# Weighting and summing two of the three w_ada blocks on VectorE instead of TensorE

## The reference

```python
c_act = jax.nn.silu(c)
mod = jnp.einsum('bd,dm->bm', c_act, w_ada[l]) + b_ada[l]
shift_m, scale_m, gate_m, shift_f, scale_f, gate_f = jnp.split(mod, N_MOD, axis=-1)
h = modulate(rms_norm(x, g_norm_mix[l]), shift_m, scale_m)
p = jnp.einsum('bsd,dk->bsk', h, w_in[l])
...
x = x + gate_m[:, None, :] * mix_out
h2 = modulate(rms_norm(x, g_norm_moe[l]), shift_f, scale_f)
moe_out = expert_choice_moe(h2, w_router[l], b_router[l], w_gate_e[l], w_up_e[l], w_down_e[l])
x = x + gate_f[:, None, :] * moe_out
```

## Time and profile before

| | us |
|---|---|
| median of three runs | 1432.08 (1430.69 to 1432.92) |
| the profiled execution | 1429.03 |
| its span | 1427.2 |
| TensorE busy | 1162.0 (81%) |
| VectorE busy | 322.9 (23%) |
| ScalarE busy | 246.1 (17%) |
| GpSimd busy | 87.7 (6%) |

### The profile page before, as it was taken

How to read it: one execution, slowest core, us unless ns; L and a number is a source line. 1 busy time by engine, 2 the same in 40 slices (tenths; PEclk the granted TensorE clock), 3 DMA queues, 4 the chain that set the end, 5 groups by cost and what they waited for, 6 DMA issues and landing times.

```text
span 1427.2 us, 16989 instructions
## 1 busy us (share of the span) xinstructions
PE 1162.0 (81%) x7070; PEld 634.3 (44%) x7071; DVE 322.9 (23%) x459; ACT 246.1 (17%) x355; POOL 87.7 (6%) x95
## 2 busy tenths in 40 slices
PE   4999999888778787777777778777787777996888
PEld 1789999533323133131222213213122223996777
DVE  1546446310000000000000000000000002666555
ACT  2423533100000000000000000000000003653644
POOL 2000000000000000000000000000000001421122
PEclk8999999697887968978787896888868889998989
DMA  9996884599999999999999999999999999742311
GB/s 333 379 361 240 265 299 174 228 421 421 422 422 421 422 421 422 422 422 422 422 422 422 422 422 422 422 422 422 422 422 422 422 422 373 242 143 89 119 64 55
DMA packets 116634, 496.33 MB, mean 348 GB/s; under 512 B 8140, under 2 KB 60772, under 8 KB 64116
## 3 DMA queue, kind: packets, MB, share of 16 engines
q1 hardware_dynamic: 114944, 490.37, 86.2%
q0 software_dynamic: 1296, 5.19, 1.1%
q10 hardware_dynamic: 356, 0.21, 0.1%
HBM read 494.70 MB, written 1.05 MB: 347 GB/s over the span
## 4 chain that ended last, share of the span: by engine, by line
DMA 45%; PE 36%; SPq 8%; DVE 4%; ACT 4%; issue 2%; POOL 0%; DVEq 0%; ACTq 0%
DMA ring<-in_w_gate_e 28%; SPq L463 8%; DMA ring<-in_w_down_e 8%; DMA ring<-in_w_up_e 7%; PE psum L556 7%; PE psum L557 6%; PE psum L558 6%; PE psum L823 6%; PE psum L804 4%; DMA ring<-in_w_in 3%; PE psum L850 2%; PE psum L624 1%; ACT ring_r L1035 1%; ACT arena L1165 1%; PE psum L675 1%
## 5 line engine op out<-in xcount | busy, mean ns | idle before, releaser
L823 PE MATMUL psum<-ring,arena 128*32 128x512 f32 x2048 | 314.6, 735 | 118.2 <-DMA ring<-in_w_gate_e 72.8
L850 PE MATMUL psum<-ring,arena 128*32 128x512 f32 x1024 | 233.0, 696 | 52.9 <-DMA ring<-in_w_down_e 38.8
L823 PEld LDWEIGHTS psum<-ring,arena 128*32 128x32 f32 x2048 | 57.3, 124 | 346.2 <-DMA ring<-in_w_gate_e 152.4
L850 PEld LDWEIGHTS psum<-ring,arena 128*32 128x32 f32 x1024 | 55.8, 121 | 220.9 <-DMA ring<-in_w_down_e 113.7
L556 PE MATMUL psum<-ring_r,ht_hi 128*128 128x256 f32 (+1 forms) x384 | 114.9, 299 | 10.9 <-DVE ht_lo L1289 7.8
L1285 DVE TENSOR_TENSOR ring_r<-ring,ring_r 128x2048 fp32r<-128x2048 f32 x43 | 101.9, 2394 | 74.0 <-ACT ring_r L1035 73.9
L556 PE MATMUL psum<-ht_hi,ring_r 128*128 128x256 f32 x384 | 109.3, 285 | 6.1 <-issue 6.1
L558 PE MATMUL psum<-ring_r,ht_lo 128*128 128x256 f32 (+1 forms) x384 | 113.2, 295 | 0.0
L557 PE MATMUL psum<-ring_r,ht_hi 128*128 128x256 f32 (+1 forms) x384 | 112.8, 294 | 0.0
L804 PEld LDWEIGHTS psum<-arena 128*128 128x128 f32 x544 | 99.9, 288 | 25.7 <-issue 24.7
L1035 ACT ACTIVATE ring_r<-ring 128x2048 fp32r<-128x2048 f32 x55 | 103.1, 1907 | 47.6 <-DMA ring<-in_w_in 30.5
(11 more groups left out here) (255 smaller groups left out, 958.0 us busy)
## 6 DMA issues: line engine op xcount, KB each, us to landing
ring<-in_w_gate_e SPq DMA_DIRECT2D x128, 1024.0 KB, 26.5
ring<-in_w_up_e SPq DMA_DIRECT2D x128, 1024.0 KB, 26.9
ring<-in_w_down_e SPq DMA_DIRECT2D x128, 1024.0 KB, 26.9
ring<-in_w_in SPq DMA_DIRECT2D x38, 1024.0 KB, 11.2
ring<-in_w_ada SPq DMA_DIRECT2D x24, 1024.0 KB, 11.0
ring<-in_w_conv_out SPq DMA_DIRECT2D x4, 1024.0 KB, 6.0
ring<-in_w_o SPq DMA_DIRECT2D x4, 1024.0 KB, 11.1
ring<-in_w_out SPq DMA_DIRECT2D x4, 1024.0 KB, 4.8
```

What stands on the lines that cost most here:

```text
L823: last = mm(psum[32 * g:32 * g + 32, b, :], cur[h][:, k, :], slot_in(s, g=4, n=512)[:, g, :], start=(k == 0), stop=(k == KD - 1), tile_pos ...
L850: last = mm(psum[32 * q:32 * q + 32, 2 + n, :], act_t[:, f % 4, (f // 4) * CAP:(f // 4 + 1) * CAP], w[:, kk, n * BANK:(n + 1) * BANK], sta ...
```

## The change

The eight slots of block 1 and of block 2 no longer go to PE. DVE multiplies each slot by its column of c_act (128 rows, one weight to a partition) and adds it to a running sum `ada_sum` of 128 x 2048 (`add_ada`): tensor_scalar for the first slot of a block, scalar_tensor_tensor in place for the seven others. It does so in unit u for the slots ahead of unit u+1, behind the splits of that unit and ahead of the emptying of its banks. PE waits at the head of unit u+1 until these additions are done (`ada_done`), and sums the 128 partitions of `ada_sum` once a block, by products with ones: `sum_row` (128x128 by 128x512) where a vector is needed as a row on all partitions, `sum_columns` (eight products with one column) where it is needed as columns. Block 1's sums stand ahead of c1's product; block 2's stand ahead of yb0's, but for one `sum_row` behind yb1. The step that makes scale_f moves on DVE from behind yb0's gating to ahead of it.

`ada_sum` takes one ring place, so arriving slots have 11 instead of 12 in the head. An ada slot is no longer released by itself: `others` adds it to the release of the first slot of the next product. The transposes of blocks 1 and 2, ACT's two copies ahead of them and the four small matmuls at L708 go.

```diff
@@ -45,7 +45,8 @@
 EXPERT_SLOTS = 24
 
 
-HEAD_PARTS, HEAD_RING = 4, RING - 4
+HEAD_PARTS, HEAD_RING = 4, RING - 5
+SUM_PLACE, HEAD_PART_ROOM = RING - 5, RING - 4
...
-        mod_rows = [area(5640, BANK), area(1536, BANK), area(2048, BANK)]
+        mod_rows = area(5640, BANK)
+        ada_sum = ring[:, SUM_PLACE, :]
...
-        part_place = {s: HEAD_RING + n % HEAD_PARTS for n, s in enumerate(head_split)}
+        part_place = {s: HEAD_PART_ROOM + n % HEAD_PARTS for n, s in enumerate(head_split)}
...
+        ada_step = {bk: n + 1 for n, bk in enumerate(bk for u in sorted(ADA_BEFORE) for bk in ADA_BEFORE[u])}
+
+        def ada_before(u):
+
+            since = max((v for v in range(u) if HEAD_UNITS[v][1]), default=-1)
+            return sum(len(ADA_BEFORE.get(v, ())) for v in range(since + 1, u + 1))
...
-            def transposed_product(s, u, act_parts):
+            def transposed_product(s, u, act_parts, others=0):
...
-                    last.then_inc(slot_used, 1)
+                    last.then_inc(slot_used, 1 if j else 1 + others)
...
+            def sum_columns(first, at):
+
+                for c in range(KD):
+                    last = mm(psum[:, 6, at + c:at + c + 1], ada_sum[:, first + c * P:first + (c + 1) * P], ones[:, 0:1], start=True, stop=True)
+                last.then_inc(ada_turned, 1)
+
+            def sum_row(first, to):
+
+                return mm(bank(to), ones, ada_sum[:, first:first + BANK], start=True, stop=True)
...
             for u, (name, slots) in enumerate(HEAD_UNITS):
                 for bk in ADA_BEFORE.get(u, ()):
-                    if bk == (1, 0):
-                        pe.wait_ge(mod_ready, 1)
-                    modulation(*bk, 3 + bk[0])
+                    pe.wait_ge(ada_done, ada_step[bk])
+                if (1, KD - 1) in ADA_BEFORE.get(u, ()):
+                    pe.wait_ge(mod_ready, 1)
+                    pe.wait_ge(gain_ready, 1)
+                    for n in range(2):
+                        sum_row(n * BANK, 4 + n).then_inc(gate_row_done, 1)
+                    sum_columns(D, 0)
+                if (2, KD - 1) in ADA_BEFORE.get(u, ()):
+                    sum_row(D + BANK, 7)
+                    sum_columns(0, KD)
...
-                    transposed_product(first_slot[name], u, (ht_hi, ht_lo))
+                    transposed_product(first_slot[name], u, (ht_hi, ht_lo), ada_before(u))
...
-                        end_first(last) if j == 0 else end_second(last, slots)
+                        end_first(last) if j == 0 else end_second(last, slots + ada_before(u))
...
-                    transposed_product(first_slot[name], u, (st_hi, st_lo))
-                    if name == "yb0":
-                        pe.wait_ge(gain_ready, 1)
-                        turn_modulation(1, 6)
-                        turn_modulation(2, 7)
+                    transposed_product(first_slot[name], u, (st_hi, st_lo), ada_before(u))
 
             pe.wait_ge(mod_ready, 2)
-            for g, b, first in ((0, 1, 0), (1, 2, 2)):
-                for n in range(2):
-                    r = 32 * (first + n)
-                    mm(bank(4 + 2 * g + n), ones[r:r + 1, :], mod_rows[b][r:r + 1, :], start=True, stop=True,
-                       tile_position=(r, 0)).then_inc(gate_row_done, 1)
+            sum_row(D, 6).then_inc(gate_row_done, 2)
...
-            def modulation_rows(b, from_bank):
-                act.wait_ge(slot_used, first_slot[f"ada{b}_{KD - 1}"] + 1)
-                f(mod_rows[b], bank(from_bank), ACT.Copy).then_inc(mod_rows_ready, 1)
-
-            modulation_rows(0, 4)
+            act.wait_ge(slot_used, first_slot[f"ada0_{KD - 1}"] + 1)
+            f(mod_rows, bank(4), ACT.Copy).then_inc(mod_rows_ready, 1)
...
-                if name == "yb0":
-                    modulation_rows(1, 4)
-                    modulation_rows(2, 5)
...
+            def summed_columns(n, q):
+                dve.wait_ge(ada_turned, n + 1)
+                link(V.tensor_tensor(mod_t[:, q:q + KD], psum[:, 6, n * KD:(n + 1) * KD], col[:, C_BADA + q:C_BADA + q + KD], ALU.add))
+
+            def add_ada(b, k):
+
+                s = first_slot[f"ada{b}_{k}"]
+                arrived(dve, s)
+                w = ring[:, place(s)[0], :]
+                if (b, k) == (2, 0):
+                    summed_columns(0, Q_SHIFT_F)
+                if k == 0:
+                    V.tensor_scalar(ada_sum, w, c_act[:, k:k + 1], None, ALU.mult).then_inc(ada_done, 1)
+                else:
+                    dve.wait_ge(ada_done, ada_step[b, k] - 1)
+                    V.scalar_tensor_tensor(ada_sum, w, c_act[:, k:k + 1], ada_sum, ALU.mult, ALU.add).then_inc(ada_done, 1)
...
                 split_ahead(head_ahead[u])
+                for bk in ADA_BEFORE.get(u + 1, ()):
+                    add_ada(*bk)
...
+                    if name == "yb0":
+                        summed_columns(1, Q_SCALE_F)
+                        V.scalar_tensor_tensor(mod_a[:, KD:2 * KD], mod_t[:, Q_SCALE_F:Q_SCALE_F + KD], 1.0, col[:, C_GMOE:C_GMOE + KD],
+                                               ALU.add, ALU.mult).then_inc(mod_ready, 1)
...
-                    if name == "yb0":
-                        modulation_columns(1, 6)
-                        modulation_columns(2, 7)
-                        V.scalar_tensor_tensor(mod_a[:, KD:2 * KD], mod_t[:, Q_SCALE_F:Q_SCALE_F + KD], 1.0, col[:, C_GMOE:C_GMOE + KD],
-                                               ALU.add, ALU.mult).then_inc(mod_ready, 1)
```

More of the change, by code:

```diff
@@ L269, in build @@
         gate_row_done, gate_row_ready = sem("gate_row_done"), sem("gate_row_ready")
+        ada_done, ada_turned = sem("ada_slots_summed"), sem("ada_sum_turned")
         squared, mean_ready, root_ready, scale_ready, xr_ready = (sem(n) for n in ("squared", "mean_ready", "root_ready", "scale_ready", "xr_ready"))
@@ L617, in turn_norm, with modulation @@
                     last.then_inc(norm_turned, 1)
-            def modulation(b, k, to):
-                s = first_slot[f"ada{b}_{k}"]
+            def modulation(k, to):
+                s = first_slot[f"ada0_{k}"]
                 arrived(pe, s)
@@ L626, in modulation, with turn_modulation @@
                 last.then_inc(slot_used, 1)
-            def turn_modulation(b, to):
-                pe.wait_ge(mod_rows_ready, b + 1)
+            def turn_modulation(to):
+                pe.wait_ge(mod_rows_ready, 1)
                 for c in range(4):
-                    last = nc.tensor.transpose(bank(to, c=4, m=P)[:, c, :], mod_rows[b][:, c * P:(c + 1) * P], ident)
+                    last = nc.tensor.transpose(bank(to, c=4, m=P)[:, c, :], mod_rows[:, c * P:(c + 1) * P], ident)
                 last.then_inc(mod_turned, 1)
+            def sum_columns(first, at):
[4 more added lines that the diff above has]
+                return mm(bank(to), ones, ada_sum[:, first:first + BANK], start=True, stop=True)
             pe.wait_ge(tables_loaded, 16)
@@ L647, in _ @@
                     nc.tensor.transpose(psum[:, 6, 0:5 + KD], vec2[0:5 + KD, :], ident[0:5 + KD, 0:5 + KD]).then_inc(gain_turned, 1)
-                modulation(0, k, 4)
-            turn_modulation(0, 5)
+                modulation(k, 4)
+            turn_modulation(5)
             for u, (name, slots) in enumerate(HEAD_UNITS):
                 for bk in ADA_BEFORE.get(u, ()):
-                    if bk == (1, 0):
-                        pe.wait_ge(mod_ready, 1)
-                    modulation(*bk, 3 + bk[0])
+                    pe.wait_ge(ada_done, ada_step[bk])
[8 more added lines that the diff above has]
+                    sum_columns(0, KD)
                 if name == "fourier_in":
@@ L1299, in split_norm, with modulation_columns @@
                     ins.then_inc(norm_lo, 1)
-            def modulation_columns(b, from_bank):
-                dve.wait_ge(mod_turned, b + 1)
+            def modulation_columns(from_bank):
+                dve.wait_ge(mod_turned, 1)
                 src = bank(from_bank, c=4, g=4, r=32)[:, :, :, 0].rearrange("p c g -> p g c")
-                at = slice(16 * b, 16 * b + 16)
-                link(V.tensor_tensor(shaped(mod_t[:, at], g=4, c=4), src, shaped(col[:, C_BADA + 16 * b:C_BADA + 16 * b + 16], g=4, c=4), ALU.add))
+                link(V.tensor_tensor(shaped(mod_t[:, 0:16], g=4, c=4), src, shaped(col[:, C_BADA:C_BADA + 16], g=4, c=4), ALU.add))
+            def summed_columns(n, q):
[12 more added lines that the diff above has]
+                    V.scalar_tensor_tensor(ada_sum, w, c_act[:, k:k + 1], ada_sum, ALU.mult, ALU.add).then_inc(ada_done, 1)
             dve.wait_ge(sig_c_ready, 1)
@@ L1321, in _ @@
             V.tensor_scalar(sub_gain, gain[:, 4:5], 1.0 - LAM_INIT, None, ALU.mult)
-            modulation_columns(0, 5)
+            modulation_columns(5)
             V.scalar_tensor_tensor(mod_a[:, 0:KD], mod_t[:, Q_SCALE_M:Q_SCALE_M + KD], 1.0, col[:, C_GMIX:C_GMIX + KD],
```

## The result

The changed kernel takes 1435.14 us (median of 8 runs, 1432.53 to 1436.46) against 1431.06 us before (8 runs, 1430.04 to 1432.92) beside it: a ratio of 1.0025, 95% interval 1.0015 to 1.0034, some 3.6 us. The profiled execution has a span of 1430.7 us, 3.5 more than the one before.

What follows compares the result with a forecast made beforehand. PE, never idle in the head, was taken as the bound. A 13.2 us PE gain less 11.0 of stalls and 0.1 at L755 gave -2.1; +3.4 for the clock made +1.3, median 1433.4 us, range 1429.0 to 1439.0.

Steps and rivals of the forecast that it cites:

- likeliest outcome: Whole kernel: time within 0.2% of before, chance 0.59, against 0.33 for slower and 0.08 for faster.
- likeliest case: Whole kernel: the forecast's own case, median 1433.4 us, between 1431.4 and 1435.4, chance 43%.
- Bound of the kernel: Head: PE is always busy and sets when the first load into a freed expert slot goes out, at 280.21 us.
- The walk: Head, start times unit by unit: PE's 13.2 us gain shrinks to 2.2 at w_o through 11.0 us of stalls.
- the small ones: Head: short PE waits for DVE's adds, 1.2 us ahead of v0, 0.6 ahead of seq01, 1.0 ahead of ga0.
- The adds: DVE in the head: fourteen adds of 2.2 us and two of 1.3, 33.4 us in all; dearer-add rival 5%.
- The clock: PE behind the v1 and gb0 stalls: 4.0 us at half clock each, costing 1.7 us each, 3.4 in all.
- The rival that it holds: PE's clock stays up behind both stalls: -2.1 us, 1430.0 us; chance 22%.
- the one of 10 us each: PE's half clock lasts 10 us behind each stall: +6.5 us, 1438.6 us; chance 20%.
- The sums on PE: Added PE work in the head: four sum_row at 0.91 us and two sum_columns at 1.7, together 7.0 us.
- The ring: Arriving slots in the head: one place fewer costs nothing; rival with a late load, 2.5 us more, 1435.9 us, chance 6%.
- L755: Product behind w_o waiting for DVE's sums: gives back up to 0.1 us of the 2.2 gained, net -2.1.

Runs made afterwards that it cites:

- all waits late: Changed kernel with PE's wait for ada_done moved from a unit's head to just ahead of the slot-releasing matmul, except at c1 and yb0: 1421.11 us, ratio 0.9927.
- filled: Changed kernel with 32 matmuls, their result never read, put ahead of the wait at v1 and at gb0: 1432.44 us, ratio 1.0003 to the kernel before.
- short adds: Changed kernel with the fourteen scalar_tensor_tensor adds cut to 8 of their 2048 columns: 1424.54 us, ratio 0.9952 to the kernel before.
- late at gb0: Changed kernel with PE's wait for ada_done moved to the slot-releasing matmul at gb0 alone: 1429.79 us, ratio 0.9986 to the kernel before.
- late at v1: Changed kernel with PE's wait for ada_done moved to the slot-releasing matmul at v1 alone: 1429.16 us, ratio 0.9980 to the kernel before.
- lambda behind: The kernel with all waits late, plus DVE's four lambda operations moved behind shift_sum: 1419.51 us, ratio 0.9911 to the kernel before.
- steps between: The kernel with lambda behind, plus eight unused modulation matmuls ahead of each of c0, v1, b0, b1, ga0 and ga1: 1426.11 us, ratio 0.9958 to the kernel before.

## Why the prediction held, and where it was off

The forecast was 1433.4 us, +1.3, with nothing measurable the likeliest outcome (0.59) and slower by over 0.2% at 0.33. It came out slower, +3.6 us with an interval of 2.1 to 4.9, whose lower part is still within 0.2%. So the likeliest outcome was narrowly missed, though the direction and the mechanism were as forecast. The measured median is 1.7 us above the forecast and inside its likeliest case's range (1431.4 to 1435.4). Some of that closeness is luck: the forecast stood on a kernel before at 1432.08 us, and the one measured beside the changed kernel was at 1431.06. In differences the forecast was 2.3 us too favourable (+1.3 against +3.6).

- **Bound of the kernel.** Right: the moment at which the queue's first load into a freed expert slot goes out carries the end. Against the 280.21 us of the earlier trace rows it moved by +3.1 us in the changed kernel and by -11.3, -0.3, -8.1, -2.3, -3.2, -11.8 and -5.0 in the kernels with all waits late, filled, with short adds, late at gb0, late at v1, with lambda behind and with steps between. The times, by the ratios, moved by +3.6, -10.4, +0.4, -6.9, -2.0, -2.9, -12.7 and -6.0: the same within 1.2 us, to both sides.
- **The walk.** v0 was computed for 54.2 and came at 54.06, seq01 66.1 and 66.12, v1 88.8 and 89.14. The two long waits were computed at 4.1 and 4.1 and were 4.40 and 4.35, the small ones at 1.2, 0.6 and 1.0 and were 1.0, 0.3 and 0.7: 11.0 and 10.75 in sum.
- **The adds.** 2.2 us taken, 2.35 measured, between the bounds of 2.0 and 3.4. The row of the same size (L1285) was the right neighbour and the small convolution times eight the wrong one. The tensor_scalar's line to 1.3 met 1.28.
- **The clock.** Taken as 4.0 us of half speed behind each wait, 3.4 us in all; it was 3.1 and 5.0, 3.5 us. That the sum fits is partly luck: the single dips cost 1.3 and 2.1 us where 1.7 was taken for each. The filled waits gave 3.1 us back and the trace 3.4. The rival that it holds is out, and so is the one of 10 us each.
- **The sums on PE.** sum_columns 1.84 us to the end of the last, 1.7 without the overlap, as at L736.
- **The ring.** Nothing measurable (0.9995), and at most 0.6 us by the interval.
- **What failed in size: a product's length on PE, and the add.** The walk came to 228.9 for w_o without the clock; with its 3.5 us, 232.4. It was 233.68. The clock accounts for none of these 1.3 us. One term is the 11.30 us of a product, which I took over unchanged: the changed kernel's v0, c0, v1, b0, c1 and b1 run at a pitch of 0.120 us instead of 0.118, 0.2 us a product. v0's share is hidden by the wait at seq01 and b1's by the one at ga0, whose start hangs on the end of c1; c0, v1, b0 and c1 make 0.6 to 0.8 us. The rest is in the three stretches where DVE sets PE's start. From the end of c0 to v1, of c1 to ga0 and of ya0 to gb0 the walk has 7.8, 12.3 and 9.7 us, and they were 8.0, 12.4 and 10.1: 0.7 us together. Four adds of 2.35 us instead of 2.2 stand in them, 0.6 us. With all waits late the first term shows with no wait beside it: c1 starts at 112.86 and yb0 at 195.48; seven products at 11.30 are 79.1 and the sums 2.6, so 0.9 us are left over, and four of the seven (c1 to ga1) have the slow pitch.
- **L755, now L774.** Taken at up to 0.1; 0.4 of waiting, and 0.6 from w_o to the experts in all. (The product with the shift sum is at L755 in the kernel before and at L774 in the changed one.) DVE's lambda operations stood ahead of the shift sum and did not move with PE: with them behind it the 0.4 went.
- **A sign that did not come.** ya0 was to start 3 us earlier than before. The walk gives that, but it leaves out the clock, and the first dip lies ahead of ya0. It started at 167.16, 0.8 us earlier. w_o was to come 1.3 us later and came 2.5 later, and the first new load at 281.5 came at 283.32.

The distance at w_o, 1.3 us, and the one behind it, 0.5, are together the whole distance between +1.3 and the +3.1 us at the first expert matmul.

## What to carry to other kernels

Work moved from a full engine to one that is half idle is free only if the full engine doesn't wait for it in order: lay the helper's work beside the other's unit by unit, and look at the short units, where the helper has no room. Put a wait as late as its reason allows; here the reason was a slot's release, and moving the wait 5.6 us back behind half a product turned +3.6 us into -10.4. And price an idle gap on TensorE at more than its length: one of 4.4 us in dense work cost 1.3 to 2.1 us of slower clock on top, while one of 2.28 us cost its length alone.

## What the runs showed of the hardware

The dip behind a wait isn't tied to its length alone: waits of 4.35, 4.40 and 4.35 us were followed by 5.0, 3.1 and 3.2 us of work at 1.2 GHz (the changed kernel's two, and the one at gb0 with v1 late), and a second one of 4.40 (v1 with gb0 late) by about 0.5 us at the full level and then 3.4 at the lower. Waits of 2.28 and 0.87 us in equally dense work were followed by no dip. That a price differs by 0.8 us between two equal waits I had not expected. Where it was highest, the mean clock was already 0.78 in the 4.30 us of the wait, so it had fallen well before the wait ended.

Sixteen f32 instructions with a single moving column take 1.84 us, no less than sixteen with 16 columns (1.85): at that size the columns cost nothing. Each of these instructions loads weights of its own. And matmuls of 128x128 by 128x256 at a granted clock of 1.00, with PE never idle, have two pitches in the same product, 0.118 and 0.120 us, each of which lasts for tens of microseconds: 11.30 or 11.48 us for 96. A product's length is thus known to 2% only; what chooses between the two I could not find.
